# A conditioning ring with two more places in its first stage, its shift steps ended at slot 48, and state blocks read from slot 54

## The reference

```python
mod = (jax.nn.silu(c) @ w_ada + b_ada)[:, None, :]          # c: 1 + 8 rows; w_ada: 2048 x 12288, f32
sh1, sc1, gt1, sh2, sc2, gt2 = jnp.split(mod, N_MOD, axis=-1)
h = rmsnorm(x, g_pre_mix) * (1.0 + sc1) + sh1
m, k_rows, v_rows, s_new = token_mixer(h, w_in, ...)        # w_in: 2048 x 6160
x = x + gt1 * rmsnorm(m, g_post_mix)
h = rmsnorm(x, g_pre_ffn) * (1.0 + sc2) + sh2
f = (jax.nn.silu(h @ w_ffn_gate) * (h @ w_ffn_up)) @ w_ffn_down
x = x + gt2 * rmsnorm(f, g_post_ffn)
```

## Time and profile before

| | |
|---|---|
| median of 3 runs | 1502.29 us (1501.54 to 1504.39) |
| the profiled execution: its own time | 1500.96 us |
| its span (first to last instruction) | 1499.2 us |
| PE busy | 1431.8 us, 96% of the span |
| DVE busy | 913.4 us, 61% |
| ACT busy | 661.2 us, 44% |
| bytes moved by DMA | 396.54 MB, 265 GB/s in the mean |
| TensorE clock granted over the span | 0.987 |

### The profile page before, as it was taken

The page is one execution under the profiler, slowest core; times in us unless marked ns, Lnnn a source line. Parts: engine busy times, 40 slices in busy tenths (PEclk is TensorE's granted clock), DMA queues, the critical chain, the costliest instruction groups (busy, mean ns, idle before and its releaser), DMA issues.

```text
span 1499.2 us, 29221 instructions
## 1 busy us (share of the span) xinstructions
PE 1431.8 (96%) x11274; PEld 1272.5 (85%) x11274; DVE 913.4 (61%) x1501; ACT 661.2 (44%) x1277; POOL 105.3 (7%) x205
## 2 busy tenths in 40 slices
PE   6779999999799999998999999999999999999997
PEld 2247787887577787796899999999999999999997
DVE  2143588995777656457656666566665665446444
ACT  1023477777556553336443434434344343334333
POOL 1000311113322200100000000000000000200000
PEclk9979999999999999999999999999999999999999
DMA  9999999999999978987765565655666656855552
GB/s 369 421 341 357 391 392 405 376 333 399 401 381 332 337 261 276 400 317 268 255 187 178 167 194 178 184 177 167 191 181 182 180 170 186 236 181 182 178 179 93
DMA packets 139043, 396.54 MB, mean 265 GB/s; under 512 B 13131, under 2 KB 17394, under 8 KB 126146
## 3 DMA queue, kind: packets, MB, share of 16 engines
q1 hardware_dynamic: 117730, 319.39, 62.6%
q0 software_dynamic: 21232, 76.10, 13.4%
HBM read 382.14 MB, written 11.21 MB: 262 GB/s over the span
## 4 chain that ended last, share of the span: by engine, by line
PE 83%; DMA 10%; DVE 3%; ACT 2%; issue 1%; POOLq 0%; POOL 0%; SPq 0%; DVEq 0%; ACTq 0%
PE ps L1907 24%; PE ps L1908 24%; PE ps L1909 24%; DMA ada_s<-in_w_ada 5%; PE ps L1841 4%; DMA v_page<-in_cache_v 2%; DMA k_page<-in_cache_k 2%; PE ps L2039 2%; PE ps L1965 1%; DMA ada_r<-in_w_ada 1%; ACT k_page L780 0%; DVE k_page L1275 0%; PE ps L2068 0%; ACT w_hi L702 0%; PE ps L2060 0%
## 5 line engine op out<-in xcount | busy, mean ns | idle before, releaser
L1907 PE MATMUL ps<-h_hi,w_hi 128*128 128x264 f32 x2304 | 665.9, 289 | 6.2 <-DVE h_lo L1213 3.6
L1908 PE MATMUL ps<-h_lo,w_hi 128*128 128x264 f32 x2304 | 656.7, 285 | 0.0
L1909 PE MATMUL ps<-h_hi,w_lo 128*128 128x264 f32 x2304 | 656.2, 285 | 0.0
L1907 PEld LDWEIGHTS ps<-h_hi,w_hi 128*128 128x128 f32 x2304 | 436.1, 189 | 51.2 <-issue 36.9
L1729 DVE TENSOR_TENSOR w_lo<-raw,w_hi 128x1024 fp32r<-128x1024 f32 x256 | 309.5, 1214 | 275.5 <-ACT w_hi L1018 274.1
L1018 ACT ACTIVATE w_hi<-raw 128x1024 fp32r<-128x1024 f32 x264 | 278.4, 1059 | 405.0 <-PE ps L1909 391.2
L1908 PEld LDWEIGHTS ps<-h_lo,w_hi 128*128 128x128 f32 x2304 | 435.5, 189 | 0.1
L1909 PEld LDWEIGHTS ps<-h_hi,w_lo 128*128 128x128 f32 x2304 | 434.4, 189 | 0.0
L1225 DVE TENSOR_TENSOR w_lo<-raw,w_hi 128x1024 fp32r<-128x1024 f32 x136 | 166.2, 1223 | 151.1 <-ACT w_hi L702 143.8
L702 ACT ACTIVATE w_hi<-raw 128x1024 fp32r<-128x1024 f32 x128 | 134.9, 1055 | 182.6 <-PE ps L1909 161.8
L1908 PE MATMUL ps<-act_lo,w_hi 128*128 (+1 forms) x704 | 200.4, 285 | 0.0
(11 more groups left out here) (336 smaller groups left out, 1205.5 us busy)
## 6 DMA issues: line engine op xcount, KB each, us to landing
ada_r<-in_w_ada SPq DMA_DIRECT2D x64, 1024.0 KB, 9.5
raw<-in_w_in SPq DMA_DIRECT2D x96, 512.0 KB, 8.9
raw<-in_w_ffn_gate SPq DMA_DIRECT2D x88, 512.0 KB, 3.7
raw<-in_w_ffn_up SPq DMA_DIRECT2D x88, 512.0 KB, 3.9
raw<-in_w_ffn_down SPq DMA_DIRECT2D x88, 512.0 KB, 4.5
ada_s<-in_w_ada SPq DMA_DIRECT2D x32, 1024.0 KB, 13.7
k_page<-in_cache_k POOLq DMA_DIRECT2D x64, 512.0 KB, 8.1
v_page<-in_cache_v POOLq DMA_DIRECT2D x38, 512.0 KB, 8.1
```

The costliest lines, as they stand in the source:

```text
L1907: mm(out, w_hi, xh, start=first, stop=False)
L1908: mm(out, w_hi, xl, start=False, stop=False)
L1909: return mm(out, w_lo, xh, start=False, stop=last)
```

## The change

It gives the first two parts of the ring two further places, 9 and 10, in memory that held the rows of `x` at the start (free once `x` has been transposed). They share the semaphores of places 7 and 8, which are used much later. The loads of steps 0 and 1 stand right behind the loads of the first four units, and those of steps 2 to 5 each move up by one pair. The steps 0 to 15 stand in slots 3 to 18, and the steps 16 to 31, which now rotate through three places (1, 9, 0), in slots 22 to 48. The first three state blocks are read at `s` = 54, 57 and 60 in place of 58, 60 and 63. POOL's two waits on the ring before the first and third K page count one step more; the step that they name was in slot 16 and slot 17 before, and is there now.

```diff
         AR = [put(f"ada_r{i}", [P, 2048], at=a) for i, a in enumerate(
-            (at_x, at_x + 8192, r0 + 38016, r0 + 46208, r0 + 71808, r0 + 80000, r0 + 88192, r0 + 54912, r0 + 63104))]
-        ADA_PLACE = [(n + 2) % 4 for n in range(16)] + [n % 2 for n in range(16)] + [2, 3, 4, 2, 3, 4, 5, 6, 3, 4, 5, 6, 4, 5, 6, 4] + \
+            (at_x, at_x + 8192, r0 + 38016, r0 + 46208, r0 + 71808, r0 + 80000, r0 + 88192, r0 + 54912, r0 + 63104,
+             r0 + 54400, r0 + 62592))]
+        ADA_PLACE = [9, 10, 2, 3, 0, 1, 9, 10, 2, 3, 0, 1, 9, 2, 3, 0] + [1, 9, 0] * 4 + [1, 0, 1, 0] + [2, 3, 4, 2, 3, 4, 5, 6, 3, 4, 5, 6, 4, 5, 6, 4] + \
                     [(7, 8, 5, 6, 4)[n % 5] for n in range(16)]
...
-        A_SLOT = {n: 3 + 9 * n // 8 for n in range(16)}
-        A_SLOT.update({16 + k: 25 + 2 * k for k in range(16)})
+        A_SLOT = {n: 3 + n for n in range(16)}
+        A_SLOT.update({16 + k: s for k, s in enumerate((22, 24, 25, 27, 29, 30, 32, 34, 35, 37, 39, 40, 42, 44, 46, 48))})
...
+            sp.wait_ge(tr_done, 2 + KC)
+            ada_load(0)
+            ada_load(1)
             sp.dma_start(WG[:, :, :], win_v[:, :, NIN * CG:NIN * CG + RANK]).then_inc(misc_in, 16)
...
             sp.wait_ge(ads_used, 2 * KC)
-            sp.wait_ge(tr_done, 2 + KC)
-            ada_load(0)
-            ada_load(1)
+            ada_load(2)
+            ada_load(3)
...
-                    ada_load(2)
-                    ada_load(3)
-                for n in range(4, 53):
-                    if n < 16 and s == A_SLOT[n - 4] + 4:
-                        ada_load(n)
-                    if 16 <= n < 18 and s == 22 + n - 16:
-                        ada_load(n)
-                    if 18 <= n < 32 and s == A_SLOT[n - 2] + 3:
+                    ada_load(4)
+                    ada_load(5)
+                for n in range(6, 53):
+                    if n < 32 and s == A_SLOT[ADA_BEFORE[n]] + 3 + (n < 18):
                         ada_load(n)
...
-                if s == 58:
+                if s == 54:
...
-                if s in (58, 60, 63):
-                    state_load((58, 60, 63).index(s))
+                if s in (54, 57, 60):
+                    state_load((54, 57, 60).index(s))
...
-            pool.wait_ge(ada_used, 13)
+            pool.wait_ge(ada_used, 14)
...
-                    pool.wait_ge(ada_used, 14)
+                    pool.wait_ge(ada_used, 15)
```

More of the change, by code:

```diff
@@ L209, in stickbreak_gla_layer @@
         AR = [put(f"ada_r{i}", [P, 2048], at=a) for i, a in enumerate(
-            (at_x, at_x + 8192, r0 + 38016, r0 + 46208, r0 + 71808, r0 + 80000, r0 + 88192, r0 + 54912, r0 + 63104))]
-        ADA_PLACE = [(n + 2) % 4 for n in range(16)] + [n % 2 for n in range(16)] + [2, 3, 4, 2, 3, 4, 5, 6, 3, 4, 5, 6, 4, 5, 6, 4] + \
+            (at_x, at_x + 8192, r0 + 38016, r0 + 46208, r0 + 71808, r0 + 80000, r0 + 88192, r0 + 54912, r0 + 63104,
+             r0 + 54400, r0 + 62592))]
+        ADA_PLACE = [9, 10, 2, 3, 0, 1, 9, 10, 2, 3, 0, 1, 9, 2, 3, 0] + [1, 9, 0] * 4 + [1, 0, 1, 0] + [2, 3, 4, 2, 3, 4, 5, 6, 3, 4, 5, 6, 4, 5, 6, 4] + \
                     [(7, 8, 5, 6, 4)[n % 5] for n in range(16)]
-        ADA_COUNT = [ADA_PLACE[:n + 1].count(p) for n, p in enumerate(ADA_PLACE)]
+        ADA_SIGNAL = [(0, 1, 2, 3, 4, 5, 6, 7, 8, 7, 8)[p] for p in ADA_PLACE]
+        ADA_COUNT = [ADA_SIGNAL[:n + 1].count(p) for n, p in enumerate(ADA_SIGNAL)]
         ADA_BEFORE = [max([m for m in range(n) if ADA_PLACE[m] == p], default=None) for n, p in enumerate(ADA_PLACE)]
@@ L396, in ada_load @@
                     sp.wait_ge(ada_used, ADA_BEFORE[n] + 1)
-                sp.dma_start(AR[p][:, :], ada_start(2 * KC + n)).then_inc(ada_in[p], 16)
+                sp.dma_start(AR[p][:, :], ada_start(2 * KC + n)).then_inc(ada_in[ADA_SIGNAL[n]], 16)
             for n in range(6, 2 * KC):
@@ L1856, in ada_next @@
                 p = ADA_PLACE[n]
-                pe.wait_ge(ada_in[p], 16 * ADA_COUNT[n])
+                pe.wait_ge(ada_in[ADA_SIGNAL[n]], 16 * ADA_COUNT[n])
                 ada_step(AR[p], n % KC, TURN_BANK[n // KC + 2]).then_inc(ada_used, 1)
```

## The result

The changed kernel takes 1510.35 us (median of 4 runs, 1505.96 to 1512.34), the kernel before in the same rounds 1502.37 us (1501.54 to 1504.39). The ratio is 1.005, with a 95% interval from 1.0038 to 1.0062: slower, by 5.7 to 9.3 us. The forecast was 1495.8 us. The profiled execution has 1509.67 us of its own and a span of 1508.0 us, 8.8 us over the span before.

What follows compares the result with a forecast made beforehand. PE was taken to bound slots 0 to 55 and DMA slots 56 to 73. Ring wait -2.2, shift's row -0.7, V pages -2.6 and clock -1.0 gave -6.5 us: 1495.8 us from 1502.29, range 1489.5 to 1502.5.

Steps and rivals of the forecast that it cites:

- ring wait: 200 to 345 us: PE's waits for ring blocks go, as three blocks are loaded ahead; -2.2 us, between 0 and -3.5.
- price of a step: Slots 22 to 55: moved steps delay PE up to 4.8 us near slot 48, made up by slot 56; 0 in sum.
- bound by PE in slots 0 to 55: Slots 0 to 55: PE sets the pace except for a few microseconds; DMA does from slot 56 to 73.
- the low part's and the evacuation's waits: 200 to 345 us: PE waits of 0.8 and 0.5 us, read as late weights, counted in the range to -3.5 us.
- The shift's row: Near 340 us: PE's wait for ACT's copy of the row goes, the last step ending seven slots ahead; -0.7 us, or 0.
- V page waits: 345 to 445 us: 1.05 MB less in the full DMA queue shortens PE's 12.7 us of waits; -2.6 us, between 0 and -6.4.
- rival 1: Behind 345 us: V pages stay at 9.3 us and PE waits longer for them; total about 1501 us; chance 0.22.
- The clock: 345 to 395 us: part of 3.3 us lost to a lower granted clock returns; -1.0 us, between 0 and -3.3.
- Loads 0 to 3 and POOL's waits: From 97 us: early loads fill the DMA hole at no cost; first K pages issued 1.2 us later, also no cost; 0.
- Rival 2: Units 28 to 38: denser ring loads collide with K pages, new PE waits and lower clock; +4.2 us, 1506.5 us; chance 0.10.
- its own rule: At 200 us: the collision begins to decide when less than one of the three extra ring blocks is ahead.

Runs made afterwards that it cites:

- experiment 9: Changed kernel with ring loads 20, 21 and 22 cut to 256 of 2048 columns, matmuls unchanged (part of the shift wrong): 1503.41 us, ratio to before 1.0008.
- Experiment 2: Changed kernel with the shift's last eight steps spread over slots 37 to 55, so steps stand in 49 to 55 again: 1506.64 us, ratio to before 1.0036.
- experiment 6: Kernel before with the matmuls of steps 28, 29, 30 (slots 49, 51, 53) cut to 32 of 512 columns: 1502.84 us, ratio 1.0000.
- experiment 7: Kernel before with the matmuls of steps 24, 25, 26 (slots 41, 43, 45) cut to 32 of 512 columns: 1499.99 us, ratio 0.9984.
- experiment 4: Changed kernel with steps 0 to 15 back in their old slots 3 to 19, and POOL's waits with them: 1508.83 us, ratio to before 1.0046.
- experiment 11: Changed kernel with the matmuls of steps 19, 20, 21 (slots 27, 29, 30) cut to 32 of 512 columns, bytes unchanged: 1512.21 us, ratio to before 1.006.
- experiment 5: Changed kernel with the three state blocks issued at units 58, 60 and 63 again, as before the change: 1511.5 us, ratio to before 1.0058.
- experiment 10: Kernel before with ring loads 29, 30 and 31 cut to 256 of 2048 columns, matmuls unchanged (part of the shift wrong): 1502.91 us, ratio 1.0002.
- experiment 1: Changed kernel's early loads and new places, but all steps at the slots of before and state blocks at 58, 60, 63: 1502.05 us, ratio to before 1.0001.
- experiment 3: Changed kernel with shift steps in slots 22, 24, 25, the rest in 35 to 55, loads at most two units ahead: 1503.53 us, ratio to before 1.001.
- experiment 8: Kernel before with the matmuls of steps 18, 19, 20 (slots 29, 31, 33) cut to 32 of 512 columns: 1501.01 us, ratio 0.9993.
- experiment 12: Early loads with first-stage steps and states as before, but shift steps at 21 to 35 (odd), 38, 41, 44, 47, 49 to 55 (odd): 1504.85 us, ratio to before 1.0016.

## Why the prediction was wrong

Two steps of it failed, and both are shown by experiments. The larger is the ring wait's, "If all three fit, the backlog in the full stretch at 225 us is as before, and the wait goes": taking the bytes of three blocks out gave back 6.9 us (experiment 9). The other is the price of a moved step.

**The price of a step, 0.** The sentence that failed reads: "At the end of slot 55 PE has done the same work ... has made it up by slot 56. The steps cost nothing in sum." PE had indeed done the same work, but a step has the same price only where PE is the bound. It costs 1.1 us between units 35 and 48 (61.8 us with 7 steps, 58.4 with 4, 64.0 with 9) and almost nothing between 48 and 56 (37.2 us with 4, 37.0 with 1), since VectorE and ScalarE set the pace there. The change took its steps out of the stretch where they were nearly free: 2.9 us by the table. Experiment 2 put three steps back from the stretch 35 to 48 into 48 to 56, and the two together got 2.3 us shorter (98.8 to 96.5); experiments 6 and 7 took the same work out of each, for 0 and 2.7 us. The sentence "bound by PE in slots 0 to 55" rested on PE waiting for nothing there. But with 2.4 us less to do there it waits 1.5 us for VectorE (experiment 6): it just did not wait, and there was no margin behind it.

**The ring wait, -2.2 us.** The wait went, the 2.2 us did not. "If all three fit, the backlog in the full stretch at 225 us is as before": they did not fit. The hole from 97 to 103 us took 0.8 MB and not 1.7 ((254 - 115) GB/s x 6 us), from 118 to 160 us the rate was 376 GB/s as before, and by 200 us SP's queue was 1.1 blocks ahead, by 225 us 2.1. Blocks 20 to 22 came 18 to 22 us earlier instead and stood in the queue ahead of the weights of units 32 to 35: +4.4 us. I had the low part's and the evacuation's waits in this term as a gain of up to 1.3 us, "both late because of weights". They were not: the rows of before show ScalarE waiting for PE (0.79 us) and VectorE (1.57 us) ahead of the evacuation at unit 32, and ahead of the one at 202 us, of the 0.5 us wait, it waited for PE alone. It was the change that made the weights late.

**The shift's row, -0.7 us.** It grew to 1.7 us. With the last step out of the way ScalarE's own order ended last: the row's copy stands behind the page sums and a high part (347.84 us), and ran at 348.79 us although the step had long been done. The prediction's bound allowed 0, not a loss. Its reading that PE waits for nothing where the rate is under 380 GB/s did not hold for this wait either: it lay in the stretch at 370 GB/s.

**The V page waits, -2.6 us.** 11.2 us in place of 12.7. But the other kernels with the change's slots for the states have 12.7, 12.4 and 11.6 us (experiments 4, 9 and 11), those with the states put back are no higher (11.0 us in experiment 5), and the stretch from unit 56 to 73 got no shorter. The step from bytes to waits, which the prediction named as the likeliest to fail, did fail, but already ahead of the waits: "behind 345 us it is 1.05 MB less" did not come about. From 345 to 400 us SP's queue moved 6.33 MB, against 6.45 before, and 6.37 in experiment 10, where 2.75 MB ahead of it had been taken out. (The last ring block was issued at 302.4 us, 24 us earlier and not 40.) So rival 1's outcome holds for this part, the V pages being as slow as before (9.2 and 9.3 us). Its reason is not shown. By the Trainium skill, page "DMA: Bandwidth & Descriptors", section "Queues, rings and completion order", the engines take turns between the queues that have work, packet by packet. From this the prediction worked out that a shorter SP queue gives POOL's pages nothing. No run here tests that behind 345 us, and from 205 to 228 us the trace of experiment 9 goes against so strict a reading: with the blocks' bytes gone from SP's queue POOL's K pages landed in 6.9 us in place of 9.2.

**The clock, -1.0 us.** It did not come. Behind 345 us, for which the term was made, PE's loss by the prediction's own reckoning is 41 x 0.08 + 50 x 0.07 = 6.8 us up to 445 us (a clock of 0.93 from 395 to 445 us, 1.00 before), in place of 3.3. Experiment 7 runs the program of before there, and its profile comes to 6.8 us as well (0.95, 0.64 and 0.97 in the three stretches), so that the change is the cause is not shown. What does belong to the change is the clock of 0.90 from 225 to 260 us, 1.8 us of it right behind the longest wait.

**Loads 0 to 3 and POOL's waits, 0.** Right by the medians: 1502.05 against 1501.96 us for the loads alone. The reason given, that whatever is issued from unit 6 on lands at about the same time, is not: unit 8's high part began at 129.0 to 130.9 us in place of 127.2 to 128.5 (experiment 1).

**Sum.** Forecast -6.5 us; the table of the trace gives +4.4 at units 32 to 35 (the lower clock in it), +2.9 from steps moved (3.1 paid, 0.2 given back), +1.3 and +0.2 behind, which the scatter covers: 8.8 us. **Rival 2** named the place, the mark and the time to 4 us: a wait for `proj_t` of over 4 us between 205 and 265 us with a clock under 1.00 was its sign, and 1506.5 us its time. It had 0.10. I put it low because "115 GB/s at 97 us is a hole beyond doubt": it was, but a hole of two blocks 100 us earlier does not decide where block 20 stands. By its own rule it should not have decided, since 1.1 blocks, not less than one, were ahead at 200 us. It put the collision at 4.2 + 3.3 us, where the table has 4.4, and came near 1510 only because it took two things over from the forecast that err the other way: the steps at no cost (2.9 us), and 3.3 us won for the row and the V pages. So it had the mechanism, and its time is in part luck.

## What to carry to other kernels

An engine that waits for nothing is not thereby the bound: before work is moved from one stage to another, take out a known 2 or 3 us in each and see where the time follows. Here the same 2.4 us were worth 2.7 us in one place and 0 in another. And of transfers that are brought forward, write out what stands behind them in the same queue: in a stretch near the full rate the price fell on the next transfers of that queue above all, and from there, through an engine that works in order, on a step that seems to have nothing to do with it.

## What the runs showed of the hardware

A single wait of PE can be followed by a lower granted clock. Behind the 5.2 us wait before unit 32 the matmuls took 0.22 us in place of 0.12 for 4.0 us. Over the stretch from 225 to 260 us, with the wait in it, the mean clock was 1.00 with 1.0 and 1.6 us of wait before unit 32 (experiment 9 and the kernel before), with 1.8 us it was 1.00 once (experiment 7) and 0.95 once (experiment 10), with 2.5 to 3.8 us it was 0.90 to 0.95 (experiments 1, 3, 4, 6, 8, 12), and with 4.6 to 6.5 us 0.90 (2, 5, 11 and the changed kernel).

Queues shared unevenly under load. From 205 to 228 us, with 6% more moved in all, a unit's weights in the crowded queue took 42% longer to land and a K page in the other queue 10%; with the blocks' bytes taken out again both got faster, the weights from 15.0 to 8.6 us and the K pages from 9.2 to 6.9 us.
